# Cross attention of a two-block kernel: three rounded passes in place of f32 for part of its products

## The chip, the cores and the metric

The kernel runs on one core of a Trainium2 chip. The metric is the device time of one execution in microseconds (us). A core has TensorE (PE, with its weight loads PEld), VectorE (DVE), ScalarE (ACT), GpSimd (POOL) and SyncE (SP), each with its own queue of instructions; they meet only in semaphores.

## The reference, cut to what matters

Two different transformer-like blocks follow one another on 256 tokens of width 1024. The change touches the second block's cross attention over 256 memory rows, 4 heads of 256 channels:

```python
def memory_cross_attention(h, m, w_q, w_kv, w_o):
    q = (h @ w_q).reshape(Bn, S, X_HEADS, X_HEAD_DIM)
    k, v = jnp.split(m @ w_kv, 2, axis=-1)
    ...
    s = jnp.einsum('bshd,bmhd->bhsm', q, k).astype(jnp.float32) * (X_HEAD_DIM ** -0.5)
    p = jax.nn.softmax(s, axis=-1).astype(v.dtype)
    o = jnp.einsum('bhsm,bmhd->bshd', p, v).reshape(Bn, S, D_MODEL)
    return o @ w_o
...
x = x + rms_norm(memory_cross_attention(rms_norm(x, pre_x_g), rms_norm(mem, mem_g), ...), post_x_g)
```

`rms_norm` divides each token by its root mean square; for the queries that is a factor for each token.

## The kernel before

All weights stream through three slots of 1 MB. SP loads a group into `raw`; ACT copies it to `high`, which rounds it (fp32r); DVE (POOL for a few groups) subtracts the two into `low`. A product with a weight is three PE passes, `mm3` (L1999): low x high, high x low, high x high. Activations are split in the same way, into `act_hl`, `hid_h` and `hid_l`. `products` (L2005) runs one chunk, 8 k-tiles in two groups (k-tiles 0 to 3 and 4 to 7), and calls extra work "at" a k-tile; in mode "C" an output tile is channels by tokens, with 256 moving columns, in mode "T" tokens by channels with 512. A chunk's output is a pair of the four banks of `wide`; the pairs alternate. Banks 4 to 7 serve the attention.

Every engine's program is one hand-written list in its own order, and that order is what matters. `ahead_of(key)` and `ahead_of_half` on ACT and DVE split the weight groups that lie two ahead of the chunk named.

Around cross attention the chunks run: `kv` 0, `zc`, `q2`, `k2`, `za`, `v2`, `kv` 1, `kv` 2, `mix_top`, `mix_bottom`, `kv` 3, `xq` 0, `xq` 1, `xo` 0, `xo` 1. Keys come from `kv` 0 (heads 0, 1) and `kv` 1 (heads 2, 3), values from `kv` 2 and `kv` 3. ACT takes each out of PSUM (`kv_in`, L1009) into `k_mem` and `v_mem`, f32.

- The queries' root of the norm: DVE makes two diagonals (`norm_diag`, L1354), PE multiplies ones with them in the midst of `xq` 0 (`rep_made`, L2272), ACT copies the result (`rep_out`, L849), and DVE multiplies the query banks with it and 1/16 (`scaled_in`, L1398) into `x_q`.
- `x_scores(i)` (L2442) are the scores of heads 2i and 2i+1, 8 products in f32; `x_scores(0)` sits at k-tile 4 of `xq` 1. DVE takes the maxima (`x_max`, L1788), ACT the exponentials with their sums (`x_exp`, L1090), DVE divides (`x_norm`, L1794), PE turns the weights (`x_turn`, L2452), ACT copies them out (`x_turned`, L1100), and `x_out(i)` (L2461) multiplies them with the values, 8 products in f32. ACT and DVE split the result into quarters of `act_hl` (`x_out`, L1105 and L1564), which `xo` reads, quarter 0 first.
- After `xq` 1 PE runs `x_turn(0)`, `x_scores(1)`, `x_out(0)`, then `xo` 0 with `x_turn(1)` at k-tile 2 and `x_out(1)` at k-tile 4.

An f32 matmul of the program is two PE records in the trace. `arena` is the one large tile from which most names here are carved, so that the trace shows `arena` for `x_q`, `k_mem`, `x_p` and others, `bank` for banks 4 to 7 and `wide` for 0 to 3. L705 is ACT's helper for every activation.

Of the kernel before, what the change touches and what calls it, by code (L numbers as in the profile page):

```python
# [14 lines left out]
P = 128  # L15
T = 256
TT = T // P
D = 1024
# [91 lines left out]
class Semaphores:  # L110


    def __init__(self, new):
# [107 lines left out]
        self.tok_used = new("tok_used")  # L221
# [21 lines left out]
        self.x_t = new("x_t")  # L243
# [16 lines left out]
def two_blocks(nc, w, out):  # L260
# [3 lines left out]
    with ctx:  # L264
# [39 lines left out]

        arena = sb("arena", [P, ARENA])
        top = [0]

        def carve(*shape):
            size = math.prod(shape)
            a = arena[:, top[0]:top[0] + size]  # L310
            top[0] += size
            assert top[0] <= ARENA, top[0]
            if len(shape) == 2:
                a = a.rearrange("p (a b) -> p a b", a=shape[0])
            if len(shape) == 3:
                a = a.rearrange("p (a b c) -> p a b c", a=shape[0], b=shape[1])
            return a


# [48 lines left out]
        k_mem = carve(KD, T)  # L368
        v_mem = carve(TT, D)
# [19 lines left out]
        x_pt = carve(4, TT, T)  # L389
        x_q = carve(KD, T)  # L390
# [309 lines left out]
        def _(act):  # L700
# [110 lines left out]
            def hidden_tok():  # L811

                for t, b in enumerate(me.pair()):
                    if t:
                        act.wait_ge(sem.w_used, me.used)
                    else:
                        act.wait_ge(sem.tok_used, 1)
                    f((h_act, h_tmp)[t], b[:, :], ACT.Relu).then_inc(sem.hid_t, 1)
# [190 lines left out]
            def kv_in(c):  # L1009
                if c < 2:  # L1010
                    copy_pair(k_mem[:, 4 * c:4 * c + 2, :], k_mem[:, 4 * c + 2:4 * c + 4, :], sem.kv_in)
                else:
                    a = (c - 2) * NB
                    copy_pair(v_mem[:, 0, a:a + NB], v_mem[:, 1, a:a + NB], sem.kv_in)
# [75 lines left out]
            def x_exp(i):  # L1090

                for h in (2 * i, 2 * i + 1):
                    act.wait_ge(sem.x_max, me.seen("x_max"))
                    for t in range(TT):
                        k = 2 * h + t
                        ins = f(x_p[:, h, t, :], bank[4 + h][:, t * T:(t + 1) * T], ACT.Exp, bias=neg_max[:, k:k + 1],
                                accum_out=soft[:, k:k + 1])
                    ins.then_inc(sem.x_p, 1)

            def x_turned(i):  # L1100
                for h in (2 * i, 2 * i + 1):
                    act.wait_ge(sem.x_turned, me.seen("x_turned"))
                    f(flat(x_pt[:, h, :, :]), bank[4 + h][:, :], ACT.Copy).then_inc(sem.x_t, 1)
# [143 lines left out]
            rep_out()  # L1247
# [39 lines left out]
        def _(dve):  # L1287
# [499 lines left out]

            def x_max(i):  # L1788
                for h in (2 * i, 2 * i + 1):
                    dve.wait_ge(sem.x_s, me.seen("x_s"))  # L1790
                    dve.tensor_reduce(neg_max[:, 2 * h:2 * h + 2], in2(bank[4 + h][:, :]), AX.X, MAX, negate=True)\
                        .then_inc(sem.x_max, 1)
# [111 lines left out]
            ahead_of_half(("kv", 0), 1)  # L1904
            ahead_of("zc", "C")
# [23 lines left out]
            low_of_bank(0, b=bank[7])  # L1929
            group_norm()  # L1930
# [11 lines left out]
            norm_diag(4)  # L1942
            ahead_of(("xq", 0), "C")
            rep_wait()
            scaled_in((x_q[:, 0:2, :], x_q[:, 2:4, :]), sem.xq_in, 1 / 16)
# [4 lines left out]
            scaled_in((x_q[:, 4:6, :], x_q[:, 6:8, :]), sem.xq_in, 1 / 16)  # L1950
# [3 lines left out]
            ahead_of_half(("xo", 0), 0)  # L1954
            x_out(1)
# [37 lines left out]
        def _(pe):  # L1993
# [238 lines left out]
            def up_by_token():  # L2232
# [3 lines left out]
                for t in range(TT):  # L2236
                    tok = slice(t * P, (t + 1) * P)
                    for g, kts in parts:
# [14 lines left out]
                        if t:  # L2253
                            ins.then_inc(sem.w_used, 1)
                        elif kts[0]:
                            ins.then_inc(sem.tok_used, 1)
                            turn_half(1, 1)
# [184 lines left out]
            def x_scores(i):  # L2442

                for h in (2 * i, 2 * i + 1):
                    pe.wait_ge(sem.xq_in, h + 1)
                    for t in range(TT):
                        for k in range(2):
                            ins = mm(bank[4 + h][:, t * T:(t + 1) * T], x_q[:, 2 * h + k, t * P:(t + 1) * P],
                                     k_mem[:, 2 * h + k, :], start=k == 0, stop=k == 1)
                    ins.then_inc(sem.x_s, 1)  # L2450
# [10 lines left out]
            def x_out(i):  # L2461
                pe.wait_ge(sem.x_t, me.seen("x_t", 2))
                for h in (2 * i, 2 * i + 1):
                    for c in range(2):
                        for m in range(2):
                            ch = slice((2 * h + c) * P, (2 * h + c + 1) * P)
                            ins = mm(bank[4 + h][:, c * T:(c + 1) * T], v_mem[:, m, ch], x_pt[:, h, m, :],
                                     start=m == 0, stop=m == 1)
# [61 lines left out]
            pe.wait_ge(sem.kv_in, 2)  # L2530
# [20 lines left out]
            pe.wait_ge(sem.kv_in, 6)  # L2551
# [7 lines left out]
            products(("xq", 0), "C", fresh=True, at={4: rep_made})  # L2559
            pe.wait_ge(sem.kv_in, 8)  # L2560
# [4 lines left out]
            products(("xo", 0), "T", fresh=True, at={2: lambda: x_turn(1), 4: lambda: x_out(1)})  # L2565
# [48 lines left out]
```

## Time and profile before

| | |
|---|---|
| median of 3 runs (764.51 to 764.67) | 764.54 us |
| profiled execution | 764.42 us |
| its span, first to last instruction | 762.7 us |
| granted PE clock, mean | 0.999 |
| PE busy | 754.1 us, 99% |
| DVE busy | 515.7 us, 68% |
| ACT busy | 400.4 us, 53% |
| POOL busy | 71.6 us, 9% |
| DMA | 135.66 MB, mean 178 GB/s |

PE has an instruction under way in 99% of the span. The ends of matmuls are modelled, so that share alone does not say that PE bounds the kernel; the chain that ended last, followed back from the last instruction, does.

### The profile page before, as it was taken

The page shows a single profiled execution, that of the slowest core. Times are in us where ns is not written, and L with a number is a line of the kernel's source. Part 1 is how long each engine was busy: PE and PEld are TensorE (multiplying, and loading weights), DVE is VectorE, ACT ScalarE, POOL GpSimd, SP SyncE. Part 2 cuts the span into 40 slices and gives each one's busy share as a digit, 9 for nine tenths or more (in the row PEclk, how much of TensorE's full clock was granted, in tenths as well). Part 3 has the DMA queues.
Part 4 walks back from the last instruction along what each step waited for, and adds up shares of the span by engine and source line. Part 5 has one row for each costly group of instructions (what it writes and reads, how often), then busy time and mean ns, then how long its engine had stood idle before and what let it go on. Part 6 is the DMA issues. An engine that isn't in the chain of part 4 may idle for free.

```text
span 762.7 us, 10445 instructions
## 1 busy us (share of the span) xinstructions
PE 754.1 (99%) x4313; PEld 655.7 (86%) x4313; DVE 515.7 (68%) x586; ACT 400.4 (53%) x506; POOL 71.6 (9%) x79
## 2 busy tenths in 40 slices
PE   9999999999999999999999999999999999999997
PEld 9988888888988888888899888789887988888885
DVE  5857965695756666565759999774647655656554
ACT  6466388543644554544653486663547533444442
POOL 3000003030000000000233322020003000000000
PEclk9999999999999999999999999999999999999999
DMA  9754565445565555665466445365235565555531
GB/s 307 230 173 160 162 224 199 133 161 173 173 234 194 169 166 168 206 215 191 173 211 193 163 139 192 113 235 177 87 114 184 171 221 202 185 179 186 167 130 56
DMA packets 74287, 135.66 MB, mean 178 GB/s; under 512 B 4458, under 2 KB 28928, under 8 KB 74240
## 3 DMA queue, kind: packets, MB, share of 16 engines
q1 hardware_dynamic: 72304, 130.80, 51.0%
q10 hardware_dynamic: 1936, 4.19, 1.7%
q8 instruction: 34, 0.56, 0.3%
q14 instruction: 13, 0.11, 0.0%
HBM read 133.93 MB, written 1.05 MB: 177 GB/s over the span
## 4 chain that ended last, share of the span: by engine, by line
PE 90%; DVE 7%; ACT 1%; issue 1%; POOL 1%; DVEq 0%; POOLq 0%; ACTq 0%
PE wide L1997 63%; PE bank L1997 24%; DVE arena L1419 3%; PE bank L2115 3%; DVE low L1303 1%; ACT arena L705 1%; POOL low L558 1%; ACT high L705 0%; DVE arena L1547 0%; DVE arena L1684 0%; DVE neg_max L1689 0%; DVE act_hl L1392 0%; DVE tiny L1655 0%; DVE xn L1775 0%; DVE x L1785 0%
## 5 line engine op out<-in xcount | busy, mean ns | idle before, releaser
L1303 DVE TENSOR_TENSOR low<-raw,high 128x2048 fp32r<-128x2048 f32 (+1 forms) x115 | 259.7, 2277 | 114.9 <-ACT high L705 112.1
L705 ACT ACTIVATE high<-raw 128x2048 fp32r<-128x2048 f32 (+1 forms) x130 | 234.3, 1821 | 127.2 <-PE wide L1997 99.1
L1997 PE MATMUL wide<-act_hl,high 128*128 128x256 f32 (+1 forms) x1184 | 297.3, 330 | 0.0
L1997 PE MATMUL wide<-act_hl,low 128*128 128x256 f32 x832 | 235.7, 283 | 0.0
L1997 PEld LDWEIGHTS wide<-act_hl,high 128*128 128x128 f32 x1184 | 199.9, 190 | 22.5
L1997 PE MATMUL wide<-high,act_hl 128*128 128x512 f32 (+1 forms) x560 | 176.3, 388 | 0.6 <-DVE act_hl L1392 0.3
L1997 PEld LDWEIGHTS wide<-act_hl,low 128*128 128x128 f32 x832 | 158.1, 190 | 1.6 <-issue 0.7
L1997 PEld LDWEIGHTS wide<-high,act_hl 128*128 128x128 f32 x560 | 104.1, 188 | 23.7 <-issue 2.0
L1997 PE MATMUL wide<-low,act_hl 128*128 128x512 f32 (+1 forms) x280 | 107.5, 384 | 0.0
L1997 PE MATMUL bank<-high,hid_l 128*128 128x512 f32 x216 | 84.7, 392 | 0.2 <-DVE hid_l L1612 0.2
L1997 PE MATMUL bank<-high,hid_h 128*128 128x512 f32 x216 | 84.3, 390 | 0.0
L1997 PE MATMUL bank<-low,hid_h 128*128 128x512 f32 x216 | 84.2, 390 | 0.0
L705 ACT ACTIVATE arena<-wide 128x512 f32<-128x512 f32 x59 | 32.7, 597 | 86.2 <-PE wide L1997 86.2
L1997 PEld LDWEIGHTS wide<-low,act_hl 128*128 128x128 f32 x280 | 52.6, 188 | 9.3
L1997 PEld LDWEIGHTS bank<-high,hid_l 128*128 128x128 f32 x216 | 40.5, 188 | 9.2 <-DVE hid_l L1612 0.6
L1997 PEld LDWEIGHTS bank<-high,hid_h 128*128 128x128 f32 x216 | 40.5, 188 | 9.0
L1997 PEld LDWEIGHTS bank<-low,hid_h 128*128 128x128 f32 x216 | 40.6, 188 | 8.0
L1593 DVE TENSOR_TENSOR arena<-wide,arena 128x512 f32<-128x512 f32 x30 | 20.7, 689 | 29.8 <-ACT arena L705 29.6
L1419 DVE SCALAR_TENSOR_TENSOR arena<-arena,dw 128x256 f32<-128x256 f32 x60 | 39.8, 705 | 0.9
L1997 PE MATMUL bank<-arena 128*128 128x256 f32 (+8 forms) x256 | 37.9, 339 | 0.0
L1997 PEld LDWEIGHTS bank<-arena 128*128 128x128 f32 (+3 forms) x256 | 31.3, 179 | 6.1 <-issue 2.1
L565 POOL TENSOR_SCALAR var<-sums 128x1 f32<-128x1 f32 x8 | 6.0, 746 | 306.4 <-ACT xn L705 210.4
(206 smaller groups left out, 659.3 us busy)
## 6 DMA issues: line engine op xcount, KB each, us to landing
raw<-in_w_ff_dram SPq DMA_DIRECT2D x32, 1024.0 KB, 5.2
raw<-in_w_in_dram SPq DMA_DIRECT2D x28, 1024.0 KB, 5.3
raw<-in_w_ffn_in_dram SPq DMA_DIRECT2D x44, 512.0 KB, 4.9
raw<-in_w_ffn_out_dram SPq DMA_DIRECT2D x11, 1024.0 KB, 6.7
raw<-in_w_xkv_dram SPq DMA_DIRECT2D x8, 1024.0 KB, 5.1
raw<-in_w_o_dram SPq DMA_DIRECT2D x4, 1024.0 KB, 5.1
raw<-in_w_out_dram SPq DMA_DIRECT2D x4, 1024.0 KB, 5.1
raw<-in_w_xq_dram SPq DMA_DIRECT2D x4, 1024.0 KB, 5.1
```

What stands on the lines that cost most here:

```text
L558: pool.tensor_tensor(part(low, g), part(raw, g), f32(part(high, g)), ALU.subtract)\
L565: pool.tensor_scalar(v, sums[:, t, 0:1], sums[:, t, 1:2], EPS, ALU.add, ALU.add)\
L705: return act.activation(dst, src, func, **k)
L1303: tt(part(low, g), part(raw, g), f32(part(high, g)), SUB).then_inc(sem.low_by_dve, 1)
L1419: ins = stt(tile_of(dst, c), window, weight(j, c), tile_of(dst, c), MUL, ADD)
L1593: tt(in2(h_low[b]), wide_of(b, 0), in2(h_low[b]), ADD).then_inc(sem.hid_sum, 1)
L1997: return pe.matmul(dst, lhs, rhs, start=start, stop=stop, skip_group_check=loose)
L2115: return pe.transpose(dst, src, ident[0:n, 0:n])
```

## The change

Keys of heads 0 and 1, all values and the turned weights are kept as a rounded part and the rest (`k_high` with the free tiles of `hid1_h` as low, `v_high` and `v_low`, `x_pt_high` and `x_pt_low`); the queries of heads 0 and 1 go into `hid_h[0]` and `hid_l[0]`. `x_scores(0)` and both `x_out` use `mm3`; `x_scores(1)` stays f32. ACT makes the high parts, DVE the low ones (`kv_low`, `xq_low`, `x_turned`). The root of the queries' norm is no longer multiplied into the queries: it is the scale of the exponential, and the maxima are multiplied with it. `norm_diag(4)`, `rep_made` and `rep_out` of this norm go. In `xo` 0, `x_turn(1)` and `x_out(1)` move from k-tiles 2 and 4 to 1 and 3. A semaphore is renamed (`tok_used`, now `tile0_used`).

```diff
...
@@ -302,12 +302,14 @@
         soft = sb("soft", [P, 16])
 
 
+        arena_at = nc.sbuf_base
         arena = sb("arena", [P, ARENA])
+        arena_r = nc.alloc_sbuf_tensor_at("arena_r", [P, ARENA], F32R, offset=arena_at)
         top = [0]
 
-        def carve(*shape):
+        def carve(*shape, home=arena):
             size = math.prod(shape)
-            a = arena[:, top[0]:top[0] + size]
+            a = home[:, top[0]:top[0] + size]
             top[0] += size
             assert top[0] <= ARENA, top[0]
             if len(shape) == 2:
@@ -316,6 +318,14 @@
                 a = a.rearrange("p (a b c) -> p a b c", a=shape[0], b=shape[1])
             return a
 
+
+        def rounded(*shape):
+
+            return carve(*shape, home=arena_r)
+
+        def k_low(kt):
+
+            return hid1_h[kt // 2][:, kt % 2, :]
 
         y = carve(6, T)
         gates = carve(TT, 3 * D)
@@ -365,8 +375,10 @@
         top[0] = 0
         spatial_w = carve(4, P)
         spatial_t = carve(4, P)
-        k_mem = carve(KD, T)
-        v_mem = carve(TT, D)
+        k_high = rounded(4, T)
+        k_mem = carve(4, T)
+        v_high = [rounded(TT, NB)]
+        v_low = [rounded(TT, NB)]
         attn = top[0]
         sc = carve(8, DIAG)
         pt = carve(4, DIAG)
@@ -386,8 +398,11 @@
         post_junk = carve(TT, D)
         top[0] = attn
         x_p = carve(4, TT, T)
-        x_pt = carve(4, TT, T)
-        x_q = carve(KD, T)
+        x_pt_high = rounded(4, TT, T)
+        x_pt_low = rounded(4, TT, T)
+        v_high.append(rounded(TT, NB))
+        v_low.append(rounded(TT, NB))
+        x_q = carve(4, T)
 
         wide = ctx.enter_context(nc.psum_tensor("wide", [P, 4, NB], F32))
         bank = [wide[:, i, :] for i in range(4)]
@@ -814,7 +829,7 @@
                     if t:
                         act.wait_ge(sem.w_used, me.used)
                     else:
-                        act.wait_ge(sem.tok_used, 1)
+                        act.wait_ge(sem.tile0_used, me.seen("tile0_used"))
                     f((h_act, h_tmp)[t], b[:, :], ACT.Relu).then_inc(sem.hid_t, 1)
 
             def hidden_turned():
@@ -1008,10 +1023,13 @@
 
             def kv_in(c):
                 if c < 2:
-                    copy_pair(k_mem[:, 4 * c:4 * c + 2, :], k_mem[:, 4 * c + 2:4 * c + 4, :], sem.kv_in)
+                    k = (k_high, k_mem)[c]
+                    copy_pair(k[:, 0:2, :], k[:, 2:4, :], sem.kv_in)
                 else:
-                    a = (c - 2) * NB
-                    copy_pair(v_mem[:, 0, a:a + NB], v_mem[:, 1, a:a + NB], sem.kv_in)
+                    copy_pair(v_high[c - 2][:, 0, :], v_high[c - 2][:, 1, :], sem.kv_in)
+
+            def xq_high():
+                copy_pair(hid_h[0][:, 0:2, :], hid_h[0][:, 2:4, :], sem.x_high, 1 / 16)
 
             def qk2_in(i):
                 d = (q2, k2)[i]
@@ -1093,14 +1111,14 @@
                     act.wait_ge(sem.x_max, me.seen("x_max"))
                     for t in range(TT):
                         k = 2 * h + t
-                        ins = f(x_p[:, h, t, :], bank[4 + h][:, t * T:(t + 1) * T], ACT.Exp, bias=neg_max[:, k:k + 1],
-                                accum_out=soft[:, k:k + 1])
+                        ins = f(x_p[:, h, t, :], bank[4 + h][:, t * T:(t + 1) * T], ACT.Exp, scale=rstd[:, 8 + t:9 + t],
+                                bias=neg_max[:, k:k + 1], accum_out=soft[:, k:k + 1])
                     ins.then_inc(sem.x_p, 1)
 
             def x_turned(i):
                 for h in (2 * i, 2 * i + 1):
                     act.wait_ge(sem.x_turned, me.seen("x_turned"))
-                    f(flat(x_pt[:, h, :, :]), bank[4 + h][:, :], ACT.Copy).then_inc(sem.x_t, 1)
+                    f(flat(x_pt_high[:, h, :, :]), bank[4 + h][:, :], ACT.Copy).then_inc(sem.x_high, 1)
 
             def x_out(i):
                 act.wait_ge(sem.w_used, me.used)
@@ -1244,7 +1262,7 @@
             norm_stat(4)
             kv_in(3)
             ahead_of(("xq", 0), "C")
-            rep_out()
+            xq_high()
             ahead_of_half(("xq", 1), 0)
             x_exp(0)
             ahead_of_half(("xq", 1), 1)
@@ -1785,11 +1803,41 @@
                         stt(x[:, t, cut], xn[:, t, cut], rstd[:, k:k + 1], x[:, t, cut], MUL, ADD)\
                             .then_inc(sem.x_ready, 1)
 
+            def kv_low(c, pair):
+
+                for i, b in enumerate(pair):
+                    dve.wait_ge(sem.kv_in, 2 * c + i + 1)
+                    if c == 0:
+                        tt(hid1_h[i][:, :, :], in2(b[:, :]), f32(k_high[:, 2 * i:2 * i + 2, :]), SUB).then_inc(sem.x_low, 1)
+                    else:
+                        tt(v_low[c - 2][:, i, :], b[:, :], f32(v_high[c - 2][:, i, :]), SUB).then_inc(sem.x_low, 1)
+
+            def xq_low():
+                for i, b in enumerate(me.pair()):
+                    dve.wait_ge(sem.x_high, me.seen("x_high"))
+                    k = slice(2 * i, 2 * i + 2)
+                    stt(hid_l[0][:, k, :], in2(b[:, :]), 1 / 16, f32(hid_h[0][:, k, :]), MUL, SUB).then_inc(sem.xq_in, 1)
+
+            def xq_plain():
+                dve.wait_ge(sem.w_used, me.used)
+                for i, b in enumerate(me.pair()):
+                    ts(x_q[:, 2 * i:2 * i + 2, :], in2(b[:, :]), 1 / 16, None, MUL).then_inc(sem.xq_in, 1)
+
+            def x_turned(i):
+                for h in (2 * i, 2 * i + 1):
+                    dve.wait_ge(sem.x_high, me.seen("x_high"))
+                    tt(flat(x_pt_low[:, h, :, :]), bank[4 + h][:, :], f32(flat(x_pt_high[:, h, :, :])), SUB)\
+                        .then_inc(sem.x_low, 1)
+
             def x_max(i):
+                if i == 0:
+                    dve.wait_ge(sem.rstd, me.seen("rstd", TT))
                 for h in (2 * i, 2 * i + 1):
+                    m = neg_max[:, 2 * h:2 * h + 2]
                     dve.wait_ge(sem.x_s, me.seen("x_s"))
-                    dve.tensor_reduce(neg_max[:, 2 * h:2 * h + 2], in2(bank[4 + h][:, :]), AX.X, MAX, negate=True)\
-                        .then_inc(sem.x_max, 1)
+                    dve.tensor_reduce(m, in2(bank[4 + h][:, :]), AX.X, MAX, negate=True).then_inc(sem.dve_step, 1)
+                    dve.wait_ge(sem.dve_step, me.step())
+                    tt(m, m, rstd[:, 8:8 + TT], MUL).then_inc(sem.x_max, 1)
 
             def x_norm(i):
                 for h in (2 * i, 2 * i + 1):
@@ -1902,6 +1950,7 @@
             ahead_of_half(("kv", 0), 0)
             norm_split(2)
             ahead_of_half(("kv", 0), 1)
+            kv_low(0, me.pair())
             ahead_of("zc", "C")
             zc_in()
             ahead_of("q2", "C")
@@ -1927,6 +1976,7 @@
             spatial()
             group_mean()
             low_of_bank(0, b=bank[7])
+            kv_low(2, me.pair())
             group_norm()
             ahead_of(("mix_top", 0), "T")
             group_silu()
@@ -1939,19 +1989,20 @@
             post_last(0)
             ahead_of(("kv", 3), "T")
             norm_split(4)
-            norm_diag(4)
+            kv_low(3, me.pair())
             ahead_of(("xq", 0), "C")
-            rep_wait()
-            scaled_in((x_q[:, 0:2, :], x_q[:, 2:4, :]), sem.xq_in, 1 / 16)
+            xq_low()
             ahead_of_half(("xq", 1), 0)
             x_max(0)
             x_norm(0)
             ahead_of_half(("xq", 1), 1)
-            scaled_in((x_q[:, 4:6, :], x_q[:, 6:8, :]), sem.xq_in, 1 / 16)
+            xq_plain()
+            x_turned(0)
             x_max(1)
             x_norm(1)
             x_out(0)
             ahead_of_half(("xo", 0), 0)
+            x_turned(1)
             x_out(1)
             ahead_of_half(("xo", 0), 1)
             post_first()
@@ -2253,7 +2304,7 @@
                         if t:
                             ins.then_inc(sem.w_used, 1)
                         elif kts[0]:
-                            ins.then_inc(sem.tok_used, 1)
+                            ins.then_inc(sem.tile0_used, 1)
                             turn_half(1, 1)
                 me.used += len(parts)
                 me.pairs += 1
@@ -2445,8 +2496,13 @@
                     pe.wait_ge(sem.xq_in, h + 1)
                     for t in range(TT):
                         for k in range(2):
-                            ins = mm(bank[4 + h][:, t * T:(t + 1) * T], x_q[:, 2 * h + k, t * P:(t + 1) * P],
-                                     k_mem[:, 2 * h + k, :], start=k == 0, stop=k == 1)
+                            kt, tok = 2 * h + k, slice(t * P, (t + 1) * P)
+                            dst = bank[4 + h][:, t * T:(t + 1) * T]
+                            if h < 2:
+                                ins = mm3(dst, hid_h[0][:, kt, tok], hid_l[0][:, kt, tok], k_high[:, kt, :], k_low(kt),
+                                          k == 0, k == 1)
+                            else:
+                                ins = mm(dst, x_q[:, kt - 4, tok], k_mem[:, kt - 4, :], start=k == 0, stop=k == 1)
                     ins.then_inc(sem.x_s, 1)
 
             def x_turn(i):
@@ -2459,13 +2515,14 @@
                     ins.then_inc(sem.x_turned, 1)
 
             def x_out(i):
-                pe.wait_ge(sem.x_t, me.seen("x_t", 2))
+                pe.wait_ge(sem.x_low, 8 + 2 * i)
                 for h in (2 * i, 2 * i + 1):
                     for c in range(2):
                         for m in range(2):
-                            ch = slice((2 * h + c) * P, (2 * h + c + 1) * P)
-                            ins = mm(bank[4 + h][:, c * T:(c + 1) * T], v_mem[:, m, ch], x_pt[:, h, m, :],
-                                     start=m == 0, stop=m == 1)
+                            a = (2 * h + c) % 4 * P
+                            ins = mm3(bank[4 + h][:, c * T:(c + 1) * T], v_high[h // 2][:, m, a:a + P],
+                                      v_low[h // 2][:, m, a:a + P], x_pt_high[:, h, m, :], x_pt_low[:, h, m, :],
+                                      m == 0, m == 1)
                     ins.then_inc(sem.x_o, 1)
 
 
@@ -2527,7 +2584,7 @@
                     products(("down1", c - 1), "F", c - 1, tile0=c == n1, first=c == 1, last=c == n1)
             products(("kv", 0), "C", is_mem=True, at={KD - 1: turn_scaled})
             products("zc", "C", fresh=True)
-            pe.wait_ge(sem.kv_in, 2)
+            pe.wait_ge(sem.x_low, 2)
             products("q2", "C")
             pe.wait_ge(sem.zc_in, 1)
             products("k2", "C")
@@ -2548,7 +2605,7 @@
             products(("mix_top", 0), "T", last=False, back_first=True, at={3: turn_gated, 0: var_and_turn})
             pe.wait_ge(sem.gn_sd, 1)
             moba_turn(1, (2, 3))
-            pe.wait_ge(sem.kv_in, 6)
+            pe.wait_ge(sem.x_low, 4)
             products(("mix_top", 1), "T", last=False)
             pe.wait_ge(sem.mo_t, me.seen("mo_t", 4))
             moba_values(1, bank[5])
@@ -2556,13 +2613,13 @@
                 products(("mix_bottom", c), "T", kt0=4, fresh=c == 0, tile0=c == 1, first=False, back_first=c == 0)
             pe.wait_ge(sem.zg, 2)
             products(("kv", 3), "T", is_mem=True, at={4: lambda: turn_all(10)})
-            products(("xq", 0), "C", fresh=True, at={4: rep_made})
-            pe.wait_ge(sem.kv_in, 8)
+            products(("xq", 0), "C", fresh=True)
+            pe.wait_ge(sem.x_low, 6)
             products(("xq", 1), "C", at={4: lambda: x_scores(0)})
             x_turn(0)
             x_scores(1)
             x_out(0)
-            products(("xo", 0), "T", fresh=True, at={2: lambda: x_turn(1), 4: lambda: x_out(1)})
+            products(("xo", 0), "T", fresh=True, at={1: lambda: x_turn(1), 3: lambda: x_out(1)})
             out_by_token()
             up_by_token()
             products(("up2", 1), "C", at={4: turn_hidden})
```

## Rows read from the trace of the kernel before

**Rows 1.** The page: busy time of the engines; the chain that ended last, by engine.
```profile
PE 754.1 (99%) x4313; PEld 655.7 (86%) x4313; DVE 515.7 (68%) x586; ACT 400.4 (53%) x506; POOL 71.6 (9%) x79
...
PE 90%; DVE 7%; ACT 1%; issue 1%; POOL 1%; DVEq 0%; POOLq 0%; ACTq 0%
```

**Rows 2.** The chain that ended last, 515 to 562 us: start, length, engine, output, line, records.
```profile
520.24 0.44 PE bank L1997 x4
520.68 11.51 PE wide L1997 x96
532.19 3.45 PE bank L1997 x16
...
541.40 0.87 PE bank L2115 x8
542.27 7.12 PE bank L1997 x32
549.39 2.94 PE wide L1997 x12
```

**Rows 3.** Timeline of DVE, 526 to 549 us: start, length, line, operation, [idle before, releaser].
```profile
526.55 1.29 DVE L1402 SCALAR_TENSOR_TENSOR arena<-wide,rep 128x512 f32<-128x512 f32 x2 [1.98 <-PE wide L1997]
...
539.26 2.29 DVE L1303 TENSOR_TENSOR low<-raw,high 128x2048 fp32r<-128x2048 f32 x1 [0.98 <-ACT high L705]
541.48 1.28 DVE L1402 SCALAR_TENSOR_TENSOR arena<-wide,rep 128x512 f32<-128x512 f32 x2
...
545.97 0.69 DVE L1791 TENSOR_REDUCE neg_max<-bank 128x2 f32<-128x512 f32 x1 [1.04 <-PE bank L1997]
...
547.75 0.17 DVE L1797 RECIPROCAL soft<-soft 128x2 f32<-128x2 f32 x1 [0.36 <-ACT arena L705]
...
548.49 0.68 DVE L1557 SCALAR_TENSOR_TENSOR act_hl<-bank,act_hl 128x512 fp32r<-128x512 f32 x1
```

**Rows 4.** Timeline of ACT, 537 to 552 us.
```profile
537.32 1.91 ACT L705 ACTIVATE high<-raw 128x2048 fp32r<-128x2048 f32 x1
541.87 1.08 ACT L705 ACTIVATE arena<-bank 128x512 f32<-128x512 f32 x2 [2.64 <-PE bank L2115]
...
546.70 0.47 ACT L705 ACTIVATE arena<-bank,neg_max 128x256 f32<-128x256 f32 x1 [0.71 <-DVE neg_max L1791]
...
547.76 0.60 ACT L705 ACTIVATE act_hl<-bank 128x512 fp32r<-128x512 f32 x1
...
549.92 1.91 ACT L705 ACTIVATE high<-raw 128x2048 fp32r<-128x2048 f32 x1
```

**Rows 5.** Timeline of DVE, 376 to 520 us: where it was idle.
```profile
398.62 0.69 DVE L1704 SCALAR_TENSOR_TENSOR arena<-arena,wide 128x512 f32<-128x512 f32 x1 [5.82 <-ACT arena L705]
...
480.24 3.35 DVE L1723 RECIPROCAL arena<-arena 128x512 f32<-128x512 f32 x1 [1.56 <-ACT arena L705]
...
517.44 2.29 DVE L1303 TENSOR_TENSOR low<-raw,high 128x2048 fp32r<-128x2048 f32 x1 [1.76 <-ACT high L705]
```

**Rows 6.** Groups by shape, ACT, then DVE: count, busy us, mean ns, idle before.
```profile
L705 ACT ACTIVATE arena<-arena,neg_max 128x256 f32<-128x256 f32 x8 | 4.0, 496 | 0.0
...
L705 ACT ACTIVATE arena<-arena,tiny 128x256 f32<-128x256 f32 x2 | 1.1, 586 | 0.0
...
L1327 DVE SCALAR_TENSOR_TENSOR tiny<-tiny 128x2 f32<-128x2 f32 x6 | 1.0, 160 | 0.2
...
L1417 DVE TENSOR_SCALAR arena<-arena,dw 128x256 f32<-128x256 f32 x2 | 0.6, 348 | 0.0
...
L1435 DVE TENSOR_SCALAR arena<-bank,if_bias 4x256 f32<-4x256 f32 x1 | 0.5, 475 | 0.9 <-PE bank L2115 0.9
...
L1492 DVE TENSOR_SCALAR arena<-arena 128x512 f32<-128x512 f32 x1 | 0.4, 415 | 0.0
```

**Rows 7.** PE's waits for other engines, 415 to 600 us: total, times, longest.
```profile
PE bank L2115 <- POOL low L558: 0.6, 1, 0.6
```

**Rows 8.** Groups by line, PE's weight loads.
```profile
L1997 PEld LDWEIGHTS wide<-act_hl,low 128*128 128x128 f32 x832 | 158.1, 190 | 1.6 <-issue 0.7
```

More of the change, by code:

```diff
@@ L220, in __init__ @@
         self.sumsq = new("sumsq")
-        self.tok_used = new("tok_used")
         self.turned = new("turned")
@@ L242, in __init__ @@
         self.x_s = new("x_s")
-        self.x_t = new("x_t")
+        self.x_high = new("x_high")
+        self.x_low = new("x_low")
         self.x_turned = new("x_turned")
```

## The prediction

> **What bounds the kernel now.** I read the page's busy times and chain first: TensorE (PE) has work in 99% of the span and 90% of the chain that ended last [rows 1]. So a microsecond saved elsewhere is worth nothing by itself, and one saved on PE is kept only if PE finds its next operands ready. Then I read the chain through cross attention piece by piece [rows 2]: there it is PE alone, from the second query chunk to the output projection. Last, I laid the DVE and ACT instructions of that stretch beside it, in order of time [rows 3, 4], to see how close behind they follow.
>
> PE's prices come from the pieces. A three-pass product of 256 columns (mode "C") is three records; 96 records took 11.51 us [rows 2], so one product costs 3 x 0.120 = 0.360 us. The f32 product of the same shape is two records; 16 records, 8 products, took 3.45 us [rows 2], or 0.431 each. The difference is 0.072 us a product (0.0715 rounded up).
>
> **PE's own saving.** Scores of heads 0 and 1 are 8 products, the weighted values of four heads 16: 24 x 0.072 = 1.72 us. The replicated root (`rep_made`) was 4 records and 0.44 us [rows 2] and goes, with DVE's two diagonals and ACT's `rep_out`, which nobody else waits for. Together 2.16 us if nothing gets in the way. Scores of heads 2 and 3 stay in f32.
>
> The Trainium skill (FP8 and Floating Point Precision, TensorE Precision Notes) says that true FP32 is four passes through the array. Read as four passes at the price of one rounded pass, a product would fall from 0.48 to 0.36 and the 24 would give 2.9 us. The rows disagree on the size: four passes took 0.431 together, so they are cheaper one by one than separate instructions, and the measured 0.072 stands.
>
> **Lows that are added before the attention.** Each is a DVE subtraction of a 128x512 bank; the nearest row, `act_hl<-bank,act_hl`, took 0.68 us [rows 3], so a pair is 1.3 to 1.4 us. `kv_low(0)` comes after the low of group zc 1: DVE has 5.82 us with nothing to do before the gate of `zc` [rows 5]. `kv_low(2)` goes between the low of bank 7 and the group norm's reciprocal, where DVE idles 1.56 us [rows 5]: it fits with 0.2 to spare. `kv_low(3)` follows ACT's copies, which end before DVE's idle 1.76 us ahead of a low is over, and the two diagonals that leave the queue there make more room [rows 5]. PE waits for these lows a whole chunk later. Cost nothing; without cover 1.37 us each on DVE, and behind them stand weight lows that PE waits for. (ACT's copies only change their output type: two into f32 took 1.08, one into fp32r 0.60 [rows 4].)
>
> **The queries.** Before, DVE took heads 0 and 1 out of PSUM in 1.29 us [rows 3], while ACT split a weight group. Now ACT copies first (2 x 0.55 to 0.60), DVE subtracts behind it, ready some 2.2 us after the chunk, and that ACT split moves 1.1 us. PE needs them half a chunk later, 11.51 / 2 = 5.75 us [rows 2], and the weight group only at `xo`. Nothing.
>
> **Softmax of heads 0 and 1, and what it pushes.** The scores start 0.44 earlier, and those of both heads end 0.44 + 8 x 0.072 = 1.01 earlier. DVE's maximum (0.69 [rows 3]) gets a dependent multiplication of 128x2 behind it: rows of that size took 0.16 [rows 6], with 0.04 between dependent steps 0.20. ACT's exponential now has two pointers, scale and bias: 128x256 from SBUF took 586 ns with two and 496 with one [rows 6], so 0.09 each and 0.18 for a head. The second head's result therefore comes 1.01 - 0.38 = 0.63 earlier, not 1.01. Behind it on ACT is the weight split of 537.32 [rows 4], behind that DVE's low of 539.26, and behind that the queries of heads 2 and 3, which DVE started at 541.48 as soon as the low let go [rows 3]. Now they start at 540.85 (`xq_plain`). PE began their scores at 542.27 [rows 2], which is no more than DVE's bank (0.68) and a handover after 541.48, so I take that start as DVE's doing and move it by the same 0.63, to 541.64. PE itself, with 0.44 + 0.57 saved, has turned heads 0 and 1 by 542.27 - 1.01 = 541.26. New wait: 0.38 us (0.3 if PE was the later of the two before).
>
> `xq_plain` is a tensor-scalar on a PSUM bank of 512, which no row shows. Bounds: 0.42 for 512 from SBUF, 0.68 for the two-tensor form from PSUM; 4x256 from PSUM took 0.475 against 0.35 for 128x256 from SBUF [rows 3, 6], so I take 0.68, as before the change. The low end would give 0.26 back.
>
> The Trainium skill (VectorE: DVE Perf Modes, Why PSUM operands drop a tier) says the same in a rule: a PSUM operand holds fp32 to one element a cycle. No 512-wide row here shows it; by the rule the wait is 0.38, by the SBUF price it would be 0.12.
>
> `x_turned(0)` (two subtractions, 1.3 us) then stands in DVE's queue ahead of `x_max(1)`. It ends by 543.4, and head 2's scores end at 541.64 + 1.72 = 543.36, so its maximum is not held up; it is head 3's that counts.
>
> **The loss that is largest.** PE runs `x_out(0)` while DVE and ACT finish the softmax of heads 2 and 3, because the low of `act_hl` quarter 0, with which the output projection starts, is queued on DVE behind `x_norm(1)`. Before, PE began both blocks at 542.27, 32 records of 0.2156 are 6.90, so it was free at 549.17 and went on at 549.39 [rows 2]: 0.22 wait. The path that released it: head 3's maximum at 545.97, exponential 546.70, reciprocal 547.75, low 548.49 [rows 3, 4]. Now that whole path starts 0.63 earlier with `x_scores(1)` and is 0.20 + 0.18 longer for head 3 (head 2's longer exponential ends before head 3's maximum is there): PE goes on at 549.39 - 0.63 + 0.38 = 549.14. But scores and `x_out(0)` now take 3.45 + 8 x 0.36 = 6.33 and end at 547.97. Wait 1.17 instead of 0.22. That is the step in which the saving of `x_out(0)` (0.57) is given back whole, and the 0.38 with it: PE is only 0.25 ahead of before here.
>
> **The rest.** Quarter 1 is copied at 548.2, ACT then splits a weight group (before from 549.92 [rows 4], now 548.7 to 550.6), DVE's low of it ends at 552.9, and only then `x_turned(1)` subtracts, to 554.2. PE does kt 0 (1.47, half of 2.94 [rows 2]), the turn (0.87), kt 1 and 2 (1.4 each), and is at `x_out(1)` at 554.28: a tie, wait 0 to 0.3, I take none. `x_out(1)` saves 0.57, and its results have kt 3 as cover. Nothing later is changed; every step there hangs on PE's end, so what is won so far stays.
>
> **Sum.** 2.16 - 0.38 - (1.17 - 0.22) = 0.83 us. The profiled execution took 764.42 (span 762.7 and 1.7 around it), so 763.6; the median of the runs, 764.54, is 0.12 above that execution, so the prediction is 763.7.
>
> **Rivals.**
> (a) PE keeps the whole 2.16: 762.4. For it: PE has no idle time in this stretch now. Against it: PE's cover in `x_out(0)` shrinks by 0.57 while the path beside it grows by 0.38. It needs DVE's and ACT's added steps to vanish in overlaps. 10%.
> (b) DVE's and ACT's queues cost more than reckoned: `x_turned(0)` delays head 2's maximum, and `x_turned(1)` comes behind a weight low that is itself late. Each would add a bank operation, 0.69, or one split-and-low step's slip: 0.7 to 0.9 of wait and 764.5. For it: both stand in queues ahead of something PE needs. 12%.
> (c) Slower, through the convolution stage: there the chain runs on DVE's taps, then POOL's root and a low of 4.6 us, for which PE waited 0.6 [rows 7]. If `kv_low(0)` ended after the gate of `zc` instead of in the idle 5.82, or its ACT copy came later, the 1.37 would reach PE in full: 764.54 + 1.37 - 0.83 = 765.1. It decides only once the idle time is under 1.4. 7%.
> (d) Slower, as the three passes do not do what they say: three weight loads a product instead of two, 0.19 us each [rows 8]. If they stopped overlapping the matmuls, a product would be 0.57 against 0.431: 24 x 0.139 = 3.34, less 0.44, so 767.4. Against it: the same loads run at a 0.120 pitch in all "C" chunks [rows 2]. 5%.
>
> **How the numbers follow.** My forecast has 66%, its own range 763.2 to 764.2 (0.26 from the tensor-scalar, 0.3 from the wait at `x_out(1)`, the rest from ends of matmuls that are modelled). About 0.2% is what a measurement of this kernel can tell from no change: 1.53 us, so faster means below 763.01, slower above 766.07. Faster: (a) and the forecast's edge, 0.14. Slower: (d) and a tail of (c), 0.06. The rest, 0.80, is the same. The range that leaves out 2 in 10 takes in (b) and most of the way to (a): 762.7 to 764.6.
>
> **What would show it.** Right: products of 0.36 where 0.431 stood in `x_scores(0)` and both `x_out`; no records of `diag`; PE idle of about 1.2 us before the first product of `xo`, released by the low of `act_hl` on DVE, and 0.4 before `x_scores(1)`, released by `xq_plain`; ACT's exponentials at 0.56; DVE's idle before `zc` and before the group norm's reciprocal shorter by 1.4, with PE's times there unchanged. Wrong: no idle before `xo` (then (a)), or waits before 500 us (then (c)), or load-bound products (then (d)).

## The result, and the profile after

The changed kernel takes 765.55 us (median of 22 runs, 765.0 to 766.34), the kernel before 764.54 in the same comparison: ratio 1.0013, 95% interval 1.0007 to 1.0019. It is about 1.0 us slower, within the 0.2% that I had called no change, but on the wrong side and outside my range (762.7 to 764.6). The profiled execution took 765.71.

The page of the kernel after: the busy times, and the chain that ended last by engine (its span is 764.0 us).

```profile
PE 752.2 (98%) x4333; PEld 654.3 (86%) x4333; DVE 522.0 (68%) x598; ACT 401.8 (53%) x507; POOL 71.5 (9%) x79
...
PE 83%; DVE 9%; ACT 2%; issue 2%; SPq 1%; DMA 1%; POOL 1%; DVEq 0%; ACTq 0%; POOLq 0%
```

PE works 1.9 us less than before. Its share of the chain falls from 90% to 83% [rows 1], but that does not measure the loss: 7% of the span would be 53 us, and the page of e1_gate below, a kernel without the loss, shows 83% too. In both the chain is followed back at its start through loads of weights. The waits of PE between 500 and 600 us do say where time goes (total, times, longest):

```profile
PE wide L2048 <- DVE act_hl L1575: 2.4, 2, 1.5
PE wide L2048 <- DVE act_hl L1410: 0.3, 2, 0.2
PE bank L2048 <- DVE arena L1824: 0.3, 1, 0.3
```

Two waits for the low of `act_hl` make 2.4 us, one of them 1.5. The one I had forecast is the smaller. The chain that ended last, from 532 us (start, length, engine, output, line, records), puts them in place:

```profile
532.09 2.85 PE bank L2048 x24
...
538.92 2.29 DVE low L1321
541.21 0.61 DVE arena L1824
...
541.86 3.73 PE bank L2048 x16
...
545.62 0.70 DVE neg_max L1838
...
549.34 1.61 PE wide L2048 x6
550.96 0.87 PE bank L2166 x8
551.83 2.75 PE wide L2048 x12
554.58 3.01 PE bank L2048 x24
557.59 1.39 PE wide L2048 x6
...
559.00 0.61 ACT act_hl L720
...
559.63 0.70 DVE act_hl L1575
...
560.46 14.54 PE wide L2048 x63
```

Read against [rows 2]: up to `xo` this is the forecast. PE comes 0.34 us late into the attention in this execution (its chain is at 453.36 where before it was at 453.02; the difference is there already at 38 us, and e5 below, with more work up to this place, is at 453.06). The first record of `xo` is at 549.34 here and was at 549.31 before; 549.31 plus 0.34 is 549.65, so PE is 0.31 ahead, where I had said 0.25. `x_out(1)` (554.58) follows without a wait in PE's list, and k-tile 3 ends at 558.97. Then PE stands still: only at 559.00, when k-tile 3 is over, does ACT copy quarter 2, DVE subtracts at 559.63, and PE goes on at 560.46. ACT's row of it, with a row of the exponentials above:

```profile
534.54 0.56 ACT L720 ACTIVATE arena<-bank,neg_max,rstd 128x256 f32<-128x256 f32 x1 [5.29 <-DVE neg_max L1840]
...
559.00 1.08 ACT L720 ACTIVATE act_hl<-bank 128x512 fp32r<-128x512 f32 x2 [6.48 <-PE wide L2048]
```

ACT was idle for 6.48 us before it and was released by `wide`, a weight product, not by `bank`, the attention's own product. PE's records at the border (start, length, [idle before, releaser]):

```profile
558.57 0.39 PE L2048 MATMUL wide<-high,act_hl 128*128 128x512 f32 x1
560.46 0.47 PE L2048 MATMUL wide<-high,act_hl 128*128 128x512 f32 x1 [1.50 <-DVE act_hl L1575]
560.77 0.40 PE L2048 MATMUL wide<-low,act_hl 128*128 128x512 f32 x1
```

A record is drawn longer than the distance at which the next one follows when nothing holds it up: these are drawn 0.39 long and 6 of them take 1.39 us in the chain, 0.23 each. So the idle time of a row, counted from a drawn end, is less than what a wait costs. From start to start, 558.57 to 560.77 is 2.20 us where two records take 0.46: the wait costs 1.74.

The chain draws a piece from the end of the one before; by first records, k-tile 4 starts at 559.16 before and at 560.46 after, 1.30 later. Less the 0.34 from the start, that is 0.96; the medians differ by 1.01.

DVE's rows (start, length, line, operation, [idle before, releaser]) for the steps around it:

```profile
398.97 0.69 DVE L1722 SCALAR_TENSOR_TENSOR arena<-arena,wide 128x512 f32<-128x512 f32 x1 [4.63 <-ACT arena L720]
...
480.60 3.35 DVE L1741 RECIPROCAL arena<-arena 128x512 f32<-128x512 f32 x1 [0.36 <-ACT arena L720]
...
517.77 2.29 DVE L1321 TENSOR_TENSOR low<-raw,high 128x2048 fp32r<-128x2048 f32 x1 [1.00 <-ACT high L720]
...
535.68 0.16 DVE L1840 TENSOR_TENSOR neg_max<-neg_max,rstd 128x2 f32<-128x2 f32 x1
...
541.12 1.28 DVE L1824 TENSOR_SCALAR arena<-wide 128x512 f32<-128x512 f32 x2
```

### The profile page after: what moved, and what is told of

It is laid out like the page before. It is cut to its first block, busy times and chain, and to the rows that moved or that the text cites. A ratio compares the mean times of both kernels' runs of the same rounds, so it can differ in the third digit from the quotient of the medians.

```text
span 764.0 us, 10498 instructions
## 1 busy us (share of the span) xinstructions
PE 752.2 (98%) x4333; PEld 654.3 (86%) x4333; DVE 522.0 (68%) x598; ACT 401.8 (53%) x507; POOL 71.5 (9%) x79
## 4 chain that ended last, share of the span: by engine, by line
PE 83%; DVE 9%; ACT 2%; issue 2%; SPq 1%; DMA 1%; POOL 1%; DVEq 0%; ACTq 0%; POOLq 0%
PE wide L2048 58%; PE bank L2048 23%; DVE arena L1437 4%; DVE low L1321 2%; PE bank L2166 2%; DMA raw<-in_w_in_dram 1%; ACT high L720 1%; ACT arena L720 1%; POOL low L573 1%; SPq L540 1%; SPq L523 1%; DVE arena L1420 0%; DVE arena L1565 0%; DVE arena L1702 0%; DVE neg_max L1707 0%
## 5 line engine op out<-in xcount | busy, mean ns | idle before, releaser
L720 ACT ACTIVATE arena<-wide 128x512 f32<-128x512 f32 x53 | 29.4, 595 | 82.8 <-PE wide L2048 82.8
L720 ACT ACTIVATE hid_h<-arena 128x512 fp32r<-128x512 f32 x27 | 16.8, 635 | 29.0 <-DVE arena L1627 16.9
L573 POOL TENSOR_TENSOR low<-raw,high 128x2048 fp32r<-128x2048 f32 x6 | 28.3, 4711 | 37.1 <-ACT high L720 37.1
```

The costliest lines, as they stand in the source:

```text
L573: pool.tensor_tensor(part(low, g), part(raw, g), f32(part(high, g)), ALU.subtract)\
L720: return act.activation(dst, src, func, **k)
```

## The experiments

Each ratio is to the kernel before on the same chip. Theory G is what the rows above suggest: `x_out` of ACT begins with `act.wait_ge(sem.w_used, me.used)`, and `ahead_of_half(("xo", 0), 0)` ahead of it has raised `me.used` by the first group of `xo`, k-tiles 0 to 3. At k-tile 4 that group is behind PE when `x_out(1)` starts; at k-tile 3 it is not. Theory Q is my rival (b), the queue of DVE.

**e1_gate.** Only that wait:

```diff
             def x_out(i):
-                act.wait_ge(sem.w_used, me.used)
+                act.wait_ge(sem.w_used, me.used - i)
```

> The changed kernel, with ACT's wait for used weight groups ahead of the copies of x_out(1) set back by one group, to that ahead of x_out(0). Theory G (the gate: with x_out(1) at k-tile 3, ACT waits for a group that PE ends only after k-tile 3): ACT copies quarter 2 during x_out(1), PE's idle of 1.50 us before k-tile 4 goes, and the time falls by 1.5 to 1.7 us, to 763.9. Theory Q (rival b: DVE's low of the turned weights stands behind a weight low and delays PE): the gate is harmless, 765.5 stays.

763.99 us, ratio 0.9991 (0.9982 to 1.0): 0.74 below the kernel before on its chip, where the changed kernel was 1.01 and, in e11, 0.93 above. ACT's timeline (start, length, operation, [idle before, releaser]) and PE's waits:

```profile
556.27 0.60 ACT L720 ACTIVATE act_hl<-bank 128x512 fp32r<-128x512 f32 x1 [3.73 <-PE bank L2048]
557.65 0.60 ACT L720 ACTIVATE act_hl<-bank 128x512 fp32r<-128x512 f32 x1 [0.78 <-PE bank L2048]
559.08 1.92 ACT L720 ACTIVATE high<-raw 128x2048 fp32r<-128x2048 f32 x1 [0.84 <-PE wide L2048]
```

```profile
PE wide L2048 <- DVE act_hl L1575: 0.9, 1, 0.9
...
PE bank L2048 <- DVE arena L1824: 0.3, 1, 0.3
```

The two copies now start 1.4 us apart, each released by `bank`, the first in the midst of `x_out(1)` and the second at its end, and the 1.5 is gone from PE's waits. Nothing else was touched, so theory G accounts for about 1.7 us; with the gate right the change is 0.7 below the kernel before, at the edge of what the interval resolves.

**e2_back.** The moved work back at its k-tiles:

```diff
-            products(("xo", 0), "T", fresh=True, at={1: lambda: x_turn(1), 3: lambda: x_out(1)})
+            products(("xo", 0), "T", fresh=True, at={2: lambda: x_turn(1), 4: lambda: x_out(1)})
```

> The changed kernel with x_turn(1) and x_out(1) at k-tiles 2 and 4 of xo 0, as before the change. Theory G: the group is used up before x_out(1) begins, so the gate costs nothing; quarter 2 is copied behind head 2's products with only head 3's 1.44 us as cover, a wait of 0.2 to 0.3; 764.1. Theory Q gives a later x_out(1) room too: also about 764.1. A theory that the loss lies elsewhere: 765.5.

764.2 us, ratio 0.9991 (0.9982 to 1.0). The chain from `xo` on:

```profile
549.65 2.97 PE wide L2048 x12
...
556.25 2.86 PE bank L2048 x24
559.11 0.04 issue
559.15 15.26 PE wide L2048 x66
```

The group is used up by 556.25, so the gate is open, and PE stands idle for 0.04 us only, as drawn. Its records at the border (start, length) show more:

```profile
558.83 0.28 PE L2048 MATMUL bank<-arena_r 128*128 128x256 f32 x1
559.15 0.50 PE L2048 MATMUL wide<-high,act_hl 128*128 128x512 f32 x1
559.48 0.40 PE L2048 MATMUL wide<-low,act_hl 128*128 128x512 f32 x1
```

They start 0.32 and 0.33 apart; in e7 below, where the operand is there in time, it is 0.12 and 0.23. That is the wait of 0.2 to 0.3 that I expected. e1 and e2 differ only in the k-tiles and in the gate, which costs nothing in either, and their times by 0.2: the move that caused the loss had no more than that to win, less than the runs resolve.

**e3_move_only.** The kernel before with only the opposite edit (k-tiles 1 and 3).

> The kernel before with nothing but the move of x_turn(1) and x_out(1) to k-tiles 1 and 3. Theory G: the move alone makes the loss, PE idles some 1.5 us before k-tile 4: 764.5 + 1.5 = 766.0. Theory Q: there are no lows of turned weights here, so nothing is late: 764.5.

766.48 us, ratio 1.0024 (1.0015 to 1.0033). Its chain:

```profile
554.78 3.46 PE bank L1997 x16
558.23 1.38 PE wide L1997 x6
...
559.64 0.61 ACT act_hl L705
...
560.27 0.70 DVE act_hl L1557
...
561.10 14.08 PE wide L1997 x61
```

The same pattern in a kernel whose cross attention has no rounded pass and no low of turned weights: k-tile 3 ends at 559.61, ACT copies, DVE subtracts, PE goes on at 561.10. The move alone costs 1.75 us. Theory Q falls with it as the cause of this loss.

**e4_gate_order.** e1, and DVE's low of the weight group two ahead goes from ahead of `xq_plain` to behind `x_out(0)`:

```diff
-            ahead_of_half(("xq", 1), 1)
+            me.used += 1
+            me.pairs += 1
             xq_plain()
...
             x_out(0)
+            split_low(chunks[("xq", 1)][1][0] + LEAD + 1)
             ahead_of_half(("xo", 0), 0)
             x_turned(1)
```

> e1_gate, and on DVE the low of the weight group two ahead stands behind x_out(0) instead of ahead of xq_plain. If the wait before x_scores(1) (0.32 us) comes from that low in DVE's queue, PE begins x_scores(1) some 0.3 us earlier and so does all that hangs on it: 0.3 below e1_gate, 763.6. If the wait comes from the end of the chunk itself, no difference.

764.74 us, ratio 0.9998 (0.9989 to 1.0007): 0.75 above e1, not 0.3 below. DVE's timeline and PE's waits:

```profile
540.64 1.29 DVE L1824 TENSOR_SCALAR arena<-wide 128x512 f32<-128x512 f32 x2 [2.78 <-PE wide L2050]
...
549.25 4.48 DVE L1321 TENSOR_TENSOR low<-raw,high 128x2048 fp32r<-128x2048 f32 x2
553.65 1.28 DVE L1829 TENSOR_TENSOR arena_r<-bank,arena_r 128x512 fp32r<-128x512 f32 x2
```

```profile
PE wide L2050 <- DVE act_hl L1575: 0.9, 1, 0.9
PE bank L2050 <- DVE arena_r L1829: 0.9, 1, 0.9
```

The wait before `x_scores(1)` is gone, as expected: `xq_plain` starts at 540.64 and `xo` at 548.87 instead of e1's 549.36, 0.4 us earlier (e1's execution came 0.08 later into the attention). But two weight lows, 4.48 us, now stand together ahead of `x_turned(1)`, whose low comes at 553.65, and `x_out(1)` waits 0.9 for it. I had moved a step without pricing what it was moved in front of. This is the mechanism of rival (b); in the changed kernel it is only just not reached.

**e7_low_between.** e4 with `x_turned(1)` between the two lows:

```diff
             split_low(chunks[("xq", 1)][1][0] + LEAD + 1)
-            ahead_of_half(("xo", 0), 0)
             x_turned(1)
+            ahead_of_half(("xo", 0), 0)
             x_out(1)
```

> e4 had PE begin xo 0.5 us earlier, but then two weight lows (4.48 us) stood together ahead of x_turned(1) on DVE and x_out(1) waited 0.87. Here one of the two stands behind x_turned(1). Theory: the 0.5 is kept and the new wait goes: 763.5. If DVE's queue is not the cause of the 0.87, 764.7 as e4.

763.34 us, ratio 0.9984 (0.9975 to 0.9993). Both parts came: PE no longer waits for `arena_r`, and the time is 0.65 below e1, 1.4 below e4 (e1 and e4 ran on another chip; with each set against the kernel before on its own, 0.6 and 1.4).

**e8_turn_in_gap.** e7, with the turn of head 2 in PE's wait ahead of `xo`:

```diff
             x_out(0)
-            products(("xo", 0), "T", fresh=True, at={1: lambda: x_turn(1), 3: lambda: x_out(1)})
+            x_turn(1, (2,))
+            products(("xo", 0), "T", fresh=True, at={1: lambda: x_turn(1, (3,)), 3: lambda: x_out(1)})
```

> e7, and the four transposes of head 2 (0.44 us) stand ahead of xo, in PE's wait of 0.9 for quarter 0, instead of at k-tile 1. If that wait is real idle time of PE, the transposes cost nothing there: 0.4 below e7, 763.1. If PE's wait is only an end of a matmul drawn too early, no difference.

763.14 us, ratio 0.9979 (0.997 to 0.9989). PE's waits:

```profile
PE wide L2050 <- DVE act_hl L1575: 0.5, 1, 0.5
PE wide L2050 <- DVE act_hl L1410: 0.3, 2, 0.2
```

The wait ahead of `xo` is 0.5 instead of 0.9: the four transposes sit in it. The medians moved by 0.2 where 0.4 was expected; their ranges overlap, so only the trace shows this step.

**e9_low_first.** e8, and on DVE quarter 0's low ahead of head 3's division:

```diff
-            x_norm(1)
-            x_out(0)
+            x_norm(1, (2,))
+            x_out(0, (0,))
+            x_norm(1, (3,))
+            x_out(0, (1,))
```

> e8, and on DVE the low of quarter 0 stands ahead of the division of head 3 instead of behind it. Theory: the 0.5 us that PE still waits before xo is this division (0.17 and 0.62) in DVE's queue; the low can go as soon as ACT has copied quarter 0, 0.25 us earlier: 762.9. The turn of head 3 comes 0.7 later and is not needed before k-tile 1. If ACT's copy is what comes last, no difference from e8, 763.1.

763.15 us, ratio 0.9978 (0.9969 to 0.9988). PE's wait there:

```profile
PE wide L2052 <- DVE act_hl L1575: 0.2, 1, 0.2
```

It fell from 0.5 to 0.2, the 0.25 expected. The time did not show it: 1.67 us below the kernel before on its chip, e8 1.56 below on its own, and the intervals are too wide to tell 0.25 from nothing. The profile does not settle it either: this one execution had a granted PE clock of 0.948 over its whole length, against 0.999 for e8, and its f32 products are longer, so only its waits can be read. Inconclusive.

**e10_before_order.** The kernel before, in f32, with e8's order on DVE and its turn of head 2 ahead of `xo`.

> The kernel before (all f32) with e8's order: on DVE the weight low two ahead stands behind x_out(0), and the four transposes of head 2 stand ahead of xo. Theory: there is only 0.22 us of PE wait there to win, as the f32 products cover the softmax: 764.3 to 764.5. If the order itself is what makes e8 fast, and not the rounded passes that it lets through, about 763.

764.76 us, ratio 1.0 (0.999 to 1.0009). The order gives nothing that these runs resolve by itself; e8's 1.6 us are the rounded passes and the root, which the order lets through. This run keeps k-tiles 2 and 4; f32 with k-tiles 1 and 3 and the gate set right was not run.

**e6_no_root.** e1 without the root's two steps (the queries' root is left out of maxima and exponential):

```diff
-                    dve.tensor_reduce(m, in2(bank[4 + h][:, :]), AX.X, MAX, negate=True).then_inc(sem.dve_step, 1)
-                    dve.wait_ge(sem.dve_step, me.step())
-                    tt(m, m, rstd[:, 8:8 + TT], MUL).then_inc(sem.x_max, 1)
+                    dve.tensor_reduce(m, in2(bank[4 + h][:, :]), AX.X, MAX, negate=True).then_inc(sem.x_max, 1)
```

and no `scale=` in `x_exp`.

> e1_gate without the queries' root in the maxima and in the exponential's scale (that factor is left out of the computation). The prediction's 0.38 us for a pair of heads (0.20 dependent multiplication, 0.18 second pointer) counts twice, before x_scores(1) and before xo: the wait of 0.32 goes and the 0.89 shrinks, 0.6 to 0.7 below e1_gate: 763.3. If the two steps vanish in overlaps, 764.0 as e1_gate.

763.53 us, ratio 0.9986 (0.9977 to 0.9995), 0.46 below e1 (0.43 when each is set against the kernel before on its chip) where I had said 0.6 to 0.7. PE's waits:

```profile
PE wide L2046 <- DVE act_hl L1575: 0.5, 1, 0.5
...
PE bank L2046 <- DVE arena_r L1829: 0.3, 1, 0.3
```

Against e1 the wait before `x_scores(1)` is gone (0.3) and that for quarter 0 is 0.5 instead of 0.9, as expected; but PE now reaches `x_out(1)` before DVE's low of the turned weights and waits 0.3 there. `xo` starts at 548.60 instead of 549.36, 0.76 earlier, which is twice the 0.38 that I had put on the two steps: the price is right, and the next wait in line takes a part back.

**e5_double_lows.** `kv_low` 0, 2 and 3 each done twice:

```diff
             kv_low(2, me.pair())
+            kv_again(2, me.pair())
```

> The changed kernel with kv_low 0, 2 and 3 done twice (the same subtraction again into the same place, and PE waits for the second). If their cover is what the prediction named (idle DVE of 4.63 us before the gate of zc, of 0.4 us before the group norm's reciprocal, of 1.0 us before a low near 517 us are left), the second kv_low(0) costs nothing, the other two push DVE by about 0.9 and 0.3 us into places where PE does not wait: 765.6 to 765.9. If these lows carry the loss (rival c: through the convolution stage), each repeats its price: 1.3 to 4 us more, with PE's waits before 500 us grown by as much.

766.44 us, ratio 1.0024 (1.0014 to 1.0033): 1.74 above the kernel before on its chip, so 0.7 to 0.8 more than the changed kernel, and more than I expected. DVE around the group norm, and PE's one new wait:

```profile
478.68 1.28 DVE L1814 TENSOR_TENSOR arena_r<-wide,arena_r 128x512 fp32r<-128x512 f32 x2
479.88 1.28 DVE L1822 TENSOR_TENSOR arena_r<-wide,arena_r 128x512 fp32r<-128x512 f32 x2
481.07 3.34 DVE L1742 RECIPROCAL arena<-arena 128x512 f32<-128x512 f32 x1
```

```profile
494.16 0.50 PE L2060 MATMUL wide<-high,act_hl 128*128 128x512 f32 x1 [0.57 <-DVE act_hl L1576]
```

The second `kv_low(2)` (479.88) pushes the reciprocal to 481.07, and the chain runs from there over the rest of the group norm and two weight lows on DVE to PE at 494.16, 0.57 us as drawn; from start to start this border takes 0.74 more than in the changed kernel (493.20 to 494.50 here, 493.48 to 494.04 there). The second `kv_low(0)` left DVE 3.43 us idle before the gate of `zc`, and PE had no wait there. So `kv_low(0)` has cover and to spare, while `kv_low(2)` had 0.36 us of it left, and not the cover further on that I had assumed.

**e11_after_again.** The changed kernel beside e9 and e10.

> The changed kernel as it is, beside the two others on the same chip. 765.5, with PE idle 0.9 us before xo and 1.5 before k-tile 4 of xo 0.

765.75 us, ratio 1.0014 (1.0005 to 1.0023), with the same two waits of PE.

## Why the prediction was wrong

Point by point, by its own steps:

- **PE's saving** held. The 24 records of `x_scores(0)` took 2.85 us, 0.356 a product against 0.360 forecast; with 0.431 before, 24 products at that pace save 1.8 us, and the 0.44 of the root went. Rival (d), load-bound products, is out. The four-pass rule of the Trainium skill (FP8 and Floating Point Precision, TensorE Precision Notes) can't be taken for a ratio of times: three rounded passes cost 83% of the f32 product here, not 75%.
- **The lows before the attention** cost nothing, as said. DVE's idle before `zc` went from 5.82 to 4.63 us, before the reciprocal from 1.56 to 0.36 [rows 5], 1.2 each where I had said 1.4, and PE waited nowhere there. Rival (c) is out; e5 shows that `kv_low(2)` was within 0.4 us of costing something.
- **The queries** of heads 0 and 1 held nobody up: PE went into their scores at 532.09 without a wait.
- **The two steps in the softmax**: the dependent multiplication took 0.16, as its neighbours did [rows 6], and the exponential 0.56 instead of 0.47 [rows 4]. e6 bears out the pair.
- **`xq_plain`**: two banks in 1.28 us, 0.68 each, the upper bound that I took, against 0.42 for the form from SBUF [rows 6]. By this row the rule of the Trainium skill (VectorE: DVE Perf Modes, Why PSUM operands drop a tier) holds. The wait before `x_scores(1)` is drawn as 0.32; from the first record of `x_turn(0)` to that of the scores it is 1.35 us (540.51 to 541.86) against 0.97 before (541.24 to 542.21), which is the 0.38 of the forecast. e4 and e7 show that it was DVE's weight low that made it.
- **The wait before `xo`** came from the path that I had named. It is drawn as 0.90; from start to start it cost 1.13 us (548.16, the last record of `x_out(0)`, to 549.65, the second of `xo`, less 0.12 and 0.23) against 1.17 forecast, and 0.16 by the same count before, where I had taken 0.22. PE was 0.31 ahead there instead of 0.25.
- **`x_turned(1)`** was the tie that I had forecast: DVE's low of it ended at 554.40. The 24 records of `x_out(1)` took 3.01 us, against 2.86 in e7, where that low stood earlier, so a wait of some 0.15 is in them and `x_out(1)` saved 0.45 of the 0.57.
- **"The rest" is the step that failed**: "`x_out(1)` saves 0.57, and its results have kt 3 as cover". `x_out(1)` itself came with no more than the 0.15 just named, but its results were not copied under k-tile 3. I had priced the move by what the moved work reads and by which DVE steps stand ahead of it. I had not asked what else ACT's copy waits for: a count of used weight groups that the first group of `xo` enters, so that moving PE's work ahead of that group's end turned a wait that was always over into one that lasts until k-tile 3 is done, and then ACT's copy (0.61), DVE's low (0.70) and their handovers lie bare. None of my rivals held this. Price: 1.74 us from start to start by the trace (1.50 as drawn), about 1.7 by e1, 1.75 by e3. My 763.7 plus 1.74 is 765.4; measured were 765.55.

With the gate set right (e1) the time was 763.99, inside the forecast's own range, and 0.74 below the kernel before where the sum had said 0.83, so the rest of the sum stands within what these runs resolve.

## What to carry to other kernels

When work is moved within one engine's program, list the waits of the engines that pick up its results, with the counts that they wait for at that place, and check each count against the new position: a wait that was always satisfied appears in no profile of before, only in the code. When a saving shortens the work under which another engine's path is hidden, that path needs its own shortening at the same time: here, with the gate set right, the passes and the root gave 0.7 us by themselves, 1.4 with DVE's list reordered (e7) and 1.6 with one turn moved into PE's wait as well (e8), and the same order without them gave nothing. And when a wait is priced from a trace, count from start to start of the records around it: as drawn, the waits here looked 0.06 to 0.24 us cheaper than they were.

## What had not been expected

e4 was the lesson a second time, on DVE: one weight low moved back by 10 us won 0.4 us at one wait and lost more at another, because it met a second one; behind `x_turned(1)` instead of ahead of it, the same low was free. And the handover of a quarter, from ACT's copy to PE's next product, is hidden almost whole under a single head's products: in e2 head 3's 1.4 us left some 0.3 of it bare.
